# Order of the first channel transform, the input's fold and split, the attention product and the last output block in an encoder layer, on one core

## The reference

```python
xn = rmsnorm(h, norm_g)
z = xn @ w_in                      # 2048 x 16384
hy_in = short_conv(hy_in, conv_w, conv_b); u, x1, x2 = jnp.split(hy_in, 3, axis=-1)
y_a = hyena_mixer(u, x1, x2, kf, skip) * jax.nn.silu(hy_gate)   # two long convolutions by FFT
y_b = fourier_mixer(fn_in) * jax.nn.silu(fn_gate)               # real part of a 2-D DFT
y_c = neighborhood_attention(q, k, v, rpb, meta_bias) * jax.nn.silu(na_gate)
m = g_a * (y_a @ w_a) + g_b * (y_b @ w_b) + g_c * (y_c @ w_c)
return rmsnorm(h + m @ w_out, final_g)[:, N_META:]
```

## Time and profile before

| | us |
|---|---|
| median of 3 runs (1165.03 to 1165.85) | 1165.55 |
| the profiled execution | 1165.13 |
| its span, from the first to the last instruction | 1163.3 |
| TensorE busy with matmuls | 1123.3 |
| VectorE busy | 766.3 |
| ScalarE busy | 561.5 |
| GpSimd busy | 63.3 |

### The profile page before, as it was taken

One profiled execution on the slowest core, in us unless ns is written; L12 is line 12 of the kernel. 1 busy time (PEld: TensorE's weight loads), 2 busy tenths in 40 slices (PEclk: granted clock), 3 DMA queues, 4 the chain that ended last, 5 costly groups with the idle time before them and its releaser, 6 DMA issues.

```text
span 1163.3 us, 17284 instructions
## 1 busy us (share of the span) xinstructions
PE 1123.3 (97%) x7222; PEld 1015.1 (87%) x7222; DVE 766.3 (66%) x1138; ACT 561.5 (48%) x771; POOL 63.3 (5%) x98
## 2 busy tenths in 40 slices
PE   4899999999999999999999999999999999999996
PEld 2798999999999989999999988888888888888885
DVE  6657788768788587886787865554554455454553
ACT  6545545455555455545555454444444434444443
POOL 4020002100020100010000000000000000000000
PEclk9999999999999999999999999999999999999998
DMA  8634433643334544435543375555555555556652
GB/s 308 226 112 156 142 143 114 203 163 134 135 131 151 189 139 145 145 119 182 181 138 124 140 270 181 191 190 198 181 187 191 199 183 181 187 203 247 232 194 96
DMA packets 30638, 201.56 MB, mean 173 GB/s; under 512 B 3888, under 2 KB 4208, under 8 KB 8016
## 3 DMA queue, kind: packets, MB, share of 16 engines
q1 hardware_dynamic: 25024, 179.63, 44.1%
q0 software_dynamic: 5248, 19.77, 5.0%
q10 hardware_dynamic: 288, 1.05, 0.2%
HBM read 195.19 MB, written 5.24 MB: 172 GB/s over the span
## 4 chain that ended last, share of the span: by engine, by line
PE 84%; DVE 9%; ACT 5%; issue 2%; DMA 0%; ACTq 0%; DVEq 0%
PE ps L563 26%; PE ps L565 26%; PE ps L564 26%; ACT w_hi L958 1%; DVE w_lo L1281 1%; PE ps L568 1%; PE ps L587 1%; DVE q_two L1479 1%; PE ps L717 0%; DVE prod L1516 0%; PE ps L606 0%; DVE prod L1517 0%; PE ps L677 0%; PE ps L607 0%; ACT q_two L1107 0%
## 5 line engine op out<-in xcount | busy, mean ns | idle before, releaser
L1281 DVE TENSOR_TENSOR w_lo<-raw,w_hi 128x1024 fp32r<-128x1024 f32 x336 | 409.7, 1231 | 288.7 <-ACT w_hi L958 287.6
L958 ACT ACTIVATE w_hi<-raw 128x1024 fp32r<-128x1024 f32 x336 | 351.2, 1057 | 371.7 <-PE ps L565 370.9
L563 PE MATMUL ps<-xn_hi,w_hi 128*128 128x272 f32 (+2 forms) x1280 | 368.3, 288 | 0.0
L565 PE MATMUL ps<-xn_hi,w_lo 128*128 128x272 f32 (+2 forms) x1280 | 366.1, 286 | 0.0
L564 PE MATMUL ps<-xn_lo,w_hi 128*128 128x272 f32 (+2 forms) x1280 | 366.0, 286 | 0.0
L563 PEld LDWEIGHTS ps<-xn_hi,w_hi 128*128 128x128 f32 x1280 | 242.8, 190 | 2.1
L564 PEld LDWEIGHTS ps<-xn_lo,w_hi 128*128 128x128 f32 x1280 | 242.6, 190 | 0.7
L565 PEld LDWEIGHTS ps<-xn_hi,w_lo 128*128 128x128 f32 x1280 | 242.7, 190 | 0.0
L563 PE MATMUL ps<-w_hi,xn_hi 128*128 128x512 f32 x384 | 152.3, 397 | 0.0
L565 PE MATMUL ps<-w_hi,xn_lo 128*128 128x512 f32 x384 | 151.0, 393 | 0.0
L564 PE MATMUL ps<-w_lo,xn_hi 128*128 128x512 f32 x384 | 150.6, 392 | 0.0
(11 more groups left out here) (244 smaller groups left out, 1359.7 us busy)
## 6 DMA issues: line engine op xcount, KB each, us to landing
raw<-w_stream SPq DMA_DIRECT2D x168, 1024.0 KB, 4.9
branch_y<-ystage POOLq DMA_DIRECT2D x12, 256.0 KB, 3.7
y_raw<-branch_y POOLq DMA_DIRECT2D x3, 1024.0 KB, 7.1
xin<-x SPq DMA_DIRECT2D x2, 1024.0 KB, 7.0
w4s<-w POOLq DMA_DIRECT2D x16, 128.0 KB, 5.8
absd<-decay POOLq DMA_DIRECT2D x8, 256.0 KB, 6.1
h<-x POOLq DMA_DIRECT2D x2, 1024.0 KB, 8.9
rows_t<-rpb POOLq DMA_DIRECT2D x8, 219.0 KB, 5.2
```

What stands on the lines that cost most here:

```text
L563: mm(out_ap, a_hi, b_hi, start=first, stop=False)
L565: return mm(out_ap, a_lo, b_hi, start=False, stop=last)
L958: A(w_hi[:, w % 2, part, :], raw[:, w % 4, 1024 * part:1024 * part + 1024], ACT.Copy).then_inc(hi_done, 1)
L1281: return V.tensor_tensor(dst, src, hi.bitcast(F32), ALU.subtract)
```

## The change

1. **Early slabs.** TensorE projects early slab 3 before `fnet_channels` 0 and 1 and not after them. Piece 2 moves from behind slab 3 to behind slab t = 0 of group 0, and `fnet_tokens` of group 0 from t = 0 to t = 1. `channels_high` and `channels_low` of group 0 move back by one slab each, and `fourier_gated(0)` on VectorE from t = 0 to t = 1, behind the copy of u.
2. **Group, t = 2.** VectorE's `fold(u)` stands before `sum_and_difference` of tile 1.
3. **Group, t = 3.** `turned` stands before the copy of q on ScalarE and VectorE.
4. **Group, t = 4.** `keep_x` of the odd filter stands at the end of t = 4, before `spectra`, and not at the start of t = 5 behind it.
5. **Group, t = 10, 12, 14.** TensorE's `attend(hh - 1)` stands before the wait for `p_done`, with waits of its own for `pt_lo` and `smax_done`.
6. **GpSimd.** `make_bias(c + 1)` moves behind three `store_y` and a `load_filter`, to the end of the group.
7. **Tail.** TensorE works the last two slabs by token tile: the 24 matmuls of tile 0, then the 24 of tile 1. The reciprocal deviation is made for each tile by itself. VectorE scales all of tile 0, which SyncE writes in one DMA; of tile 1 VectorE scales one half and ScalarE the other, written by SyncE and ScalarE.

```diff
@@ sync
-            for half in range(2):
-                cols = slice(half * D // 2, (half + 1) * D // 2)
-                sp.wait_ge(f_done, half + 1)
-                sp.dma_start(out[0:128, cols], hg[:, 0, cols]).then_inc(out_written, 16)
-            sp.wait_ge(out_written, 64)
+            sp.wait_ge(f_done, 1)
+            sp.dma_start(out[0:128, :], hg[:, 0, :]).then_inc(out_written, 16)
+            sp.wait_ge(f_done, 2)
+            sp.dma_start(out[128:256, 0:D // 2], hg[:, 1, 0:D // 2]).then_inc(out_written, 16)
+            sp.wait_ge(out_written, 48)
@@ gpsimd
-                pool.wait_ge(smax_done, (c + 1) * HC)
-                make_bias(c + 1)
                 store_y(c, 0, ya_done)
                 store_y(c, 2, yc_done)
                 load_filter(2 * c + 3)
                 store_y(c + 1, 1, yb_done)
+                pool.wait_ge(smax_done, (c + 1) * HC)
+                make_bias(c + 1)
@@ tensor
             proj_slab(2, 2, 0, NM)
+            proj_slab(3, 2, 1, NM)
             pe.wait_ge(proj_read, 1)
             pe.wait_ge(table_landed["fch"], 32)
             fnet_channels(0, 4)
             fnet_channels(1, 5)
-            proj_slab(3, 2, 1, NM)
-            pe.wait_ge(zeroed, 5)
-            pe.wait_ge(n1_lo, 1)
-            fnet_channels(2, 4)
             pe.wait_ge(table_landed["filt"], 32)
             filter_x(0)
             filter_y(0)
...
                     if t == 0:
                         if c == 0:
+                            pe.wait_ge(zeroed, 5)
+                            pe.wait_ge(n1_lo, 1)
+                            fnet_channels(2, 4)
+                        filter_f(2 * c)
+                    if t == 1:
+                        if c == 0:
                             pe.wait_ge(table_landed["ftok"], 32)
                             pe.wait_ge(n1_lo, 3)
                             fnet_tokens()
-                        filter_f(2 * c)
-                    if t == 1:
...
                         hh = (t - 8) // 2
+                        pe.wait_ge(pt_lo, c * HC + hh)
+                        pe.wait_ge(smax_done, c * HC + hh + 1)
+                        attend(hh - 1)
                         pe.wait_ge(p_done, c * HC + hh + 1)
-                        attend(hh - 1)
                         turn_p()
...
+            def last_slabs(pair):
+                for tt in range(2):
+                    toks = slice(128 * tt, 128 * tt + 128)
+                    for q in (2, 3):
+                        for kh in range(2):
+                            if tt == 0:
+                                pe.wait_ge(mlo_done, q + 1)
+                                pe.wait_ge(lo_done, 2 * (NW - 4 + q) + kh + 1)
+                            for kk in range(2):
+                                k = 4 * q + 2 * kh + kk
+                                cols = slice(WB * kk, WB * kk + WB)
+                                last = three(ps[:, pair + tt, :], m_hi[:, k, toks], m_lo[:, k, toks],
+                                             w_hi[:, q % 2, kh, cols], w_lo[:, q, kh, cols], False, k == KT - 1)
+                    last.then_inc(out_mm, 1)
@@ scalar
-                    if at_ == (5, 0):
+                    if at_ == (4, 2):
                         keep_x(a)
...
-                if p == 2:
-                    channels_high(0, False)
                 if p == 3:
                     act.wait_ge(zeroed, 5)
+                    channels_high(0, False)
                     evac(-1, "fgate", 9)
-                    channels_high(0, True)
...
+                    if t == 3:
+                        turned(c * 3 + 1, t_hi, uT_hi[:, 0:2, :], uT_hi[:, 2, :], 4, t_mm)
                     if t % 2 and BLOCKS[t // 2][0] != "v" and (c < LAST or t not in (15, 19)):
                         evac(c, BLOCKS[t // 2][0], t // 2)
-                    if t == 3:
-                        turned(c * 3 + 1, t_hi, uT_hi[:, 0:2, :], uT_hi[:, 2, :], 4, t_mm)
@@ vector
-                    filter_step(c, t, 2)
...
                     if t == 2:
                         dve.wait_ge(proj_read, blocks_read(c, "u"))
                         if c:
                             dve.wait_ge(t_mm, c * 3)
                         fold(u)
+                    filter_step(c, t, 2)
...
+            reciprocal_deviation(0)
+            dve.wait_ge(hg_done, 2 * JW - 1)
+            V.tensor_scalar(hg[:, 0, :], hg[:, 0, :], stat[:, 6:7], None, ALU.mult).then_inc(f_done, 1)
+            add_block(JW - 1, 1)
+            reciprocal_deviation(1)
             dve.wait_ge(hg_done, 2 * JW)
+            V.tensor_scalar(hg[:, 1, 0:D // 2], hg[:, 1, 0:D // 2], stat[:, 7:8], None, ALU.mult).then_inc(f_done, 1)
```

More of the change, by code:

```diff
@@ L936, in _ @@
                         w += 1
+            def last_slabs(pair):
[12 more added lines that the diff above has]
+                    last.then_inc(out_mm, 1)
             for i in range(JW):
                 pair = pair_free(("out", i))
-                for q in range(4):
+                for q in range(4 if i < JW - 1 else 2):
                     pe.wait_ge(mlo_done, q + 1)
@@ L946, in _ @@
                         turn_merged(JW - 1)
+            last_slabs(pair)
         @block.scalar
@@ L1221, in _ @@
                         spectra(c, (2,), 1)
+                    if t == 0 and c == 0:
+                        channels_high(0, True)
                     if t in (16, 17) and c < LAST:
@@ L1263, in _ @@
                 squares(JW - 1, tt)
-            act.wait_ge(f_var, 1)
-            A(stat[:, 8:10], stat[:, 4:6], ACT.Sqrt).then_inc(f_std, 1)
-            act.wait_ge(f_rstd, 1)
-            for half in range(2):
-                cols = slice(half * D // 2, (half + 1) * D // 2)
-                A(hg[:, 1, cols], hg[:, 1, cols], ACT.Copy, scale=stat[:, 7:8]).then_inc(f1_done, 1)
-            for half in range(2):
-                cols = slice(half * D // 2, (half + 1) * D // 2)
-                act.wait_ge(f1_done, half + 1)
-                act.dma_start(out[128:256, cols], hg[:, 1, cols]).then_inc(out_written, 16)
+                act.wait_ge(f_var, tt + 1)
+                A(stat[:, 8 + tt:9 + tt], stat[:, 4 + tt:5 + tt], ACT.Sqrt).then_inc(f_std, 1)
+            act.wait_ge(f_rstd, 2)
+            act.wait_ge(hg_done, 2 * JW)
+            A(hg[:, 1, D // 2:], hg[:, 1, D // 2:], ACT.Copy, scale=stat[:, 7:8]).then_inc(f1_done, 1)
+            act.wait_ge(f1_done, 1)
+            act.dma_start(out[128:256, D // 2:], hg[:, 1, D // 2:]).then_inc(out_written, 16)
         @block.vector
@@ L1602, in _ @@
                     evac(-1, "fin", 7)
-                if p == 2:
-                    channels_low(0, False)
                 if p == 3:
                     dve.wait_ge(zeroed, 5)
+                    channels_low(0, False)
                     evac(-1, "fgate", 9)
-                    channels_low(0, True)
             for c in range(0, CH):
@@ L1617, in _ @@
                     split(slab_of(c, t) + 2, 1)
-                    filter_step(c, t, 2)
-                    if t in (9, 11, 13):
-                        normalized(c, (t - 7) // 2)
-                    if t % 2 and (c < LAST or t not in (15, 19)):
-                        evac(c, BLOCKS[t // 2][0], t // 2)
-                    if t == 0 and c == 0:
-                        fourier_gated(0, 2)
                     if t == 2:
@@ L1629, in _ @@
                         fold(u)
+                    filter_step(c, t, 2)
+                    if t in (9, 11, 13):
+                        normalized(c, (t - 7) // 2)
                     if t == 3:
                         turned(c * 3 + 1, t_hi, t_lo, uT_lo[:, :, :], uT_hi[:, 0:2, :], uT_hi[:, 2, :], 4)
+                    if t % 2 and (c < LAST or t not in (15, 19)):
+                        evac(c, BLOCKS[t // 2][0], t // 2)
+                    if t == 0 and c == 0:
+                        channels_low(0, True)
+                    if t == 1 and c == 0:
+                        fourier_gated(0, 2)
                     if t == 4:
@@ L1719, in add_block @@
                     dve.wait_ge(h_landed, 48)
-                if tt == 0:
-                    dve.wait_ge(out_mm, i + 1)
+                if tt == 0 or i == JW - 1:
+                    dve.wait_ge(out_mm, i + tt + 1)
                 else:
```

19 lines of the change are left out of this document (9 added, 10 removed).

## The result

The changed kernel takes **1158.44 us** (median of 5 runs: 1155.4, 1155.9, 1158.44, 1158.62, 1159.3) where the kernel before takes 1165.55 (5 runs). The ratio is 0.9932, with a 95% interval of 0.9921 to 0.9943. So it is faster by 7.1 us between the medians (7.9 us or 0.7% between the means, which the ratio goes by), and not by the 11.5 us that I forecast; the median lies 1.2 us above my range. The five times fall into two groups with a gap of 2.5 us between them, which the kernel before does not show, and that turned out to be one part of the miss. The execution that was profiled took 1155.4 us (span 1153.6), so it is of the lower group.

A forecast was written before the change was run, and what follows sets the result against it. TensorE was busy 1123.3 of 1163.3 us, so only waits, tail and clock could be won. Terms 3.3 + 0.85 + 3 x 0.4 + 3.5 + 2.6 = 11.5 us off 1165.55 gave 1154.0, range 1149.5 to 1157.2.

The forecast's parts named there:

- The bias table of group 0: Group 0, table beside VectorE's sum and difference: a delay of 0.8 us, bounds 0 to 1.9, leaving group 0 gaining 0.85.
- The clock in the early wait: Before the first filter product: a new wait of 2.7 us leaves the clock up; if it falls, 1.7 is lost.
- rival D: Clock falls in the 2.7 us wait and group 0's table costs 1.9: 1156.8 us (1156 to 1159), chance 0.11.
- full 1.9: Group 0: the upper bound, in us, on what its bias table costs VectorE.
- The early slabs: Before group 0's scores: the filter product starts 4.05 us earlier; gain 3.3, bounds 1.6 to 6.0.
- the wait before the filter product: TensorE, early slabs: a new wait of 2.7 us for `sd_rest` before the first filter product.
- 4.95 in the forecast: Stretch from L606 to group 0's scores: the forecast gain in us without its 0.8 for the table.
- my 1.7 for the clock: Early slabs: of the 3.3 us gain, some 1.7 is the shorter wait and the rest clock; 1.7 lost if it falls.
- Parts 2 to 4: Groups 1 to 3: k copies end 0.46 us later and hold TensorE; gain 0.4 per group, bounds 0 to 2.3.
- Parts 5 and 6: Groups 0 to 2: waits for attention weights and last head's output go; gain 3 x 1.15 = 3.5 us, bounds 2.5 to 4.
- The tail: Kernel end: only 1 MB left to write where 2 MB took 5.18 us; gain 2.6, bounds 2.0 to 3.2.

The follow-up runs named there:

- the second batch: The changed kernel run once more, unaltered, beside the kernel before: 1156.54 us, ratio 0.9933.
- with eight: Changed kernel with GpSimd's four additions of the first bias table made a second time right behind the first: 1159.83 us, ratio 0.9958.
- With the table out of the way: Changed kernel with group 0's bias table built by GpSimd before the first store, not behind it: 1153.17 us, ratio 0.9899.

## Why the forecast was wrong

The parts alone were worth 1.6 (early), 0.6 (2 to 4), 0.4 (5), 3.8 (6) and 2.5 (7) by their medians, each to about 1 us: 8.9 together, and the whole change 8.8 in the second batch. Within that uncertainty they add up, so no loss between the parts shows; single terms were wrong.

**The bias table of group 0: the step that failed.** "I take 0.8, for two splits and some small operations", with bounds of 0 to 1.9. It cost 3.4, and both my value and my bound came from the earlier trace rows, where the first of two long splits began *before* the table and VectorE and GpSimd took turns, VectorE losing 1.9 in all and GpSimd 2.0 (5.64 for additions that take 3.64). Taken singly, that first split kept its 1.22 while GpSimd's first addition, begun 0.19 behind it, lasted 1.84; the second split, begun inside that addition, lasted 1.97. In group 0 GpSimd came first, by 0.08 us, and VectorE lost everything while GpSimd lost nothing. The bound that I should have taken is the whole run of the additions, 3.64: in both lengths tried, the operation waited until GpSimd's additions were through. With the 3.4 that it cost, the sum would have been 2.6 higher, 1156.6. The signs were in the earlier trace rows (two engines lengthened at once) and in the order of the program; I asked which operations would stand beside the table and not for how long one of them could be shut out.

The Trainium skill (GPSIMD Engine Reference, Specifications) puts GpSimd's SBUF interfaces down as shared with VectorE, in contention with instructions that have two SBUF inputs. The trace agrees on which operation is hit: `sd<-hm` has two inputs in SBUF. It is the length (3.85 with four additions, 7.44 with eight) that neither my working nor that sentence had.

**The clock in the early wait.** The forecast took the clock to stay up behind a wait of 2.7 us, and named the other outcome in rival D at 1.7 us. The wait came at 2.6 and the clock did fall to 0.50 behind it, in the two profiles of it, both with a late start. Where TensorE had already met the lower level near 38 us, the wait shrank to about 1.2, and the clock held behind it in four profiles of five. The first costs 2.7 us over the second. Three of the five runs were of the upper group, and so is their median; which group the median falls in is luck (in the second batch it was the lower one). Rival D (1156 to 1159) combined this with the table's "full 1.9" and so contains the result; I gave it 0.11. Its two conditions were not independent mishaps: both hang on part 1, which moves TensorE, VectorE and the release of GpSimd together.

**The early slabs otherwise**: the wait before the filter product was right (2.6 for 2.7). With the table out of the way, the stretch to the scores of group 0 was 4.8 shorter than in the profile of before, against 4.95 in the forecast. That agreement is partly luck. Beside the four other profiles with the early slabs as before, in which the clock was low for 6.8 us there and not for 3.4, the gain is 6.0 to 6.3; my 1.7 for the clock came from the one profile with the short stretch.

**Parts 2 to 4**: right in mechanism. The k copies hold TensorE in every group (1.64 against 1.5 in the forecast), `sd_rest` takes 0.5 and not 0.4. Both sizes were a little off in the same direction, so that 0.2 and not 0.4 remained in a group; over groups 1 to 3 that is 0.6 of the sum.

**Parts 5 and 6**: that the table was the whole cause of both waits was right. I had 3.5; part 6 alone gave 3.8, a period of 155.5 for 156.9 us. The two waits make 1.15 of this 1.35, and I found no row for the other 0.2. In the changed kernel a period is 155.4.

**The tail**: 2.6 in the forecast, 2.5 alone and 2.5 in the trace. The shape is as worked out (ScalarE 1.15 for its half where I had 1.1, and 2.6 us for the last 1 MB).

**Still open** is what decides whether the clock is at 0.50 near 38 us. The wait of 1.1 us stands just before it in all fourteen profiles of this study. The clock fell there in those where L606 started at 37.9 us or earlier, except one (37.75, parts 2 to 4 alone), and in none of those with 38.4 or later. No run set that start on purpose.

## What to carry to other kernels

When a step moves VectorE's work, look also for what it releases: an unchanged list on GpSimd can start at another moment, and if a VectorE operation with two SBUF inputs comes a moment behind it, price that operation at the whole length of GpSimd's run and not at some share. The price of a wait is not only its length: read the granted clock behind it in more than one execution, and if the times fall into two groups, try to fill the wait with matmuls, which cost nothing here because something behind it waits anyway. And where several products of a late engine are each waited for, their order moves the wait and does not remove it.

## What the hardware showed that I had not expected

- A VectorE operation of 0.42 us stood for 3.85 us beside four GpSimd additions (3.64) and for 7.44 beside eight (7.22), and GpSimd ran at its usual 0.90 an addition. In the earlier trace rows, where VectorE's long splits had begun 0.19 before GpSimd, and with the table early, where one had begun 0.7 before it, both engines lengthened and no operation of VectorE lasted over 2 us. So who comes first fits all of these places; the shape of the operations, which differs too, was not tried apart from it.
- The same wait in the same program ended with the granted clock at 1.00 when it was 1.24 long, and at 0.50 for the next 6 us when it was 2.62 long; but in one execution (part 5 taken out) a wait of 1.2 was followed by 0.50 from 62 to 65 us:

```profile
58.00:62.00 4.00, 2.78 (x24) 0.96 0.68 231
62.00:65.00 3.00, 3.00 (x15) 0.50 0.10 41
65.00:68.00 3.00, 3.00 (x26) 0.99 0.00 0
```

So the length of the last wait alone does not tell the clock. The Trainium skill (TensorE: Matmul & The Clock Gate, Part 1: The HAM clock gate) says that the gate goes by how busy the engine has been recently. The two executions with waits of 1.2 agree with it in this much, that equal waits ended differently.
